# Layout of the down-projection rows, the turn of the expert product, and the order of two steps in the SSD mixer

## What is computed

```python
def expert_block(args):              # for each of the 32 experts of a layer
    xb, e = args
    hb = jax.nn.silu(xb @ w_gate[e]) * (xb @ w_up[e])   # 1024 -> 512
    return hb @ w_down[e]                               # 512 -> 1024

# end of the Mamba-2 mixer, 8 groups of 256 channels
yg = yg * lax.rsqrt(jnp.mean(yg * yg, axis=-1, keepdims=True) + RMS_EPS)
y = yg.reshape(bsz, seq, D_INNER) * norm_w
return y @ out_proj
```

## Time and profile before

| | us |
|---|---|
| median of 3 runs (lowest, highest) | 1404.52 (1402.73, 1405.75) |
| the profiled execution, its own time | 1403.31 |
| its span, first to last instruction | 1401.2 |
| busy: PE, PEld, DVE, ACT, POOL | 1093.9, 731.6, 434.8, 262.1, 6.9 |
| mean granted TensorE clock | 0.869 of 2.4 GHz |
| moved by DMA | 468.16 MB, mean 334 GB/s |

### The profile page before, as it was taken

One profiled execution on the slowest core, in us unless ns is written; L12 is line 12 of the kernel. 1 busy time (PEld: TensorE's weight loads), 2 busy tenths in 40 slices (PEclk: granted clock), 3 DMA queues, 4 the chain that ended last, 5 costly groups with the idle time before them and its releaser, 6 DMA issues.

```text
span 1401.2 us, 21348 instructions
## 1 busy us (share of the span) xinstructions
PE 1093.9 (78%) x9381; PEld 731.6 (52%) x9384; DVE 434.8 (31%) x1098; ACT 262.1 (19%) x621; POOL 6.9 (0%) x28
## 2 busy tenths in 40 slices
PE   8999786677658677679999998878667576676775
PEld 7888543443424244248888887644334242343532
DVE  2241442212212122224655554452112122222123
ACT  2210111111111111113433323211111111111112
POOL 1000000000000000000000000000000000000000
PEclk9999997978879778879999999989788787878878
DMA  9753599999999999954567652469999999999993
GB/s 345 233 221 153 238 420 423 420 420 423 419 420 422 420 420 418 417 181 124 193 225 241 228 193 98 189 265 419 419 423 420 420 423 420 419 422 420 420 410 161
DMA packets 112901, 468.16 MB, mean 334 GB/s; under 512 B 16940, under 2 KB 56104, under 8 KB 96168
## 3 DMA queue, kind: packets, MB, share of 16 engines
q1 hardware_dynamic: 112304, 466.11, 83.4%
q10 hardware_dynamic: 504, 0.67, 0.1%
HBM read 465.68 MB, written 1.08 MB: 333 GB/s over the span
## 4 chain that ended last, share of the span: by engine, by line
PE 40%; issue 36%; DMA 17%; SPq 3%; DVE 2%; ACT 1%; POOL 0%; DVEq 0%; POOLq 0%; ACTq 0%
DMA w_gu<-in_expert_w_up 15%; PE pb L1164 10%; PE pa L1164 7%; PE acc L1188 4%; PE pa L1402 4%; SPq L294 3%; DMA w_x<-in_expert_w_up 2%; PE wa L1402 2%; PE acc L1290 2%; PE wb L1411 2%; PE pb L1393 2%; PE pb L1219 1%; ACT arena L448 1%; PE wa L1171 1%; PE acc L1421 1%
## 5 line engine op out<-in xcount | busy, mean ns | idle before, releaser
L1402 PE MATMUL pa<-w_gu,arena 128*32 128x256 f32 x1536 | 131.2, 516 | 80.4 <-DMA w_gu<-in_expert_w_up 80.4
L959 DVE TENSOR_SCALAR arena<-arena 128x128 f32<-128x128 f32 x64 | 14.5, 227 | 501.6 <-ACT arena L448 501.6
L448 ACT ACTIVATE arena<-wb 32x256 f32<-32x256 f32 (+3 forms) x327 | 116.8, 357 | 230.2 <-PE wb L1485 124.6
L1402 PE MATMUL wa<-w_gu,arena 128*32 128x256 f32 x1344 | 101.2, 468 | 53.6 <-DMA w_gu<-in_expert_w_up 52.0
L1402 PEld LDWEIGHTS pa<-w_gu,arena 128*32 128x32 f32 x1536 | 61.3, 147 | 144.7 <-DMA w_gu<-in_expert_w_up 85.5
L1164 PE MATMUL pb<-hnT,w_x 128*128 128x256 f32 x512 | 113.7, 380 | 2.4 <-DVE arena L999 2.4
L1164 PEld LDWEIGHTS pb<-hnT,w_x 128*128 128x128 f32 x512 | 96.9, 191 | 15.7 <-issue 2.8
L1402 PEld LDWEIGHTS wa<-w_gu,arena 128*32 128x32 f32 x1344 | 49.0, 134 | 99.9 <-DMA w_gu<-in_expert_w_up 54.4
L1393 PE MATMUL pb<-arena,hs 128*128 128x128 f32 x480 | 74.4, 319 | 31.8 <-issue 15.1
L1393 PEld LDWEIGHTS pb<-arena,hs 128*128 128x128 f32 x480 | 68.5, 227 | 45.9 <-issue 41.2
L1411 PE MATMUL wb<-w_dn,arena 128*32 128x256 f32 x1440 | 87.0, 383 | 2.2 <-ACT arena L448 2.2
(11 more groups left out here) (278 smaller groups left out, 1216.0 us busy)
## 6 DMA issues: line engine op xcount, KB each, us to landing
w_dn<-in_expert_w_down SPq DMA_DIRECT2D x45, 2048.0 KB, 27.3
w_gu<-in_expert_w_gate SPq DMA_DIRECT2D x45, 2048.0 KB, 31.5
w_gu<-in_expert_w_up SPq DMA_DIRECT2D x45, 2048.0 KB, 30.6
arena<-in_expert_w_down SPq DMA_DIRECT2D x20, 2048.0 KB, 27.7
w_x<-in_expert_w_gate SPq DMA_DIRECT2D x20, 2048.0 KB, 32.0
w_x<-in_expert_w_up SPq DMA_DIRECT2D x20, 2048.0 KB, 30.5
w_x<-in_odd_in_proj SPq DMA_DIRECT2D x16, 1024.0 KB, 5.4
w_x<-in_odd_in_proj SPq DMA_DIRECT2D x16, 512.0 KB, 5.5
```

The source lines that it names most:

```text
L448: return nc.scalar.activation(*a, **k)
L1402: ins = mm(gu[32 * j:32 * j + 32, :, :], xb[:, k, c0:c0 + CAP], w_gu[s][:, :, k, P * j:P * j + P], start=(k == 0), stop=(k == KC - 1))
```

## The change

The down weights are loaded as `(p j)`: partition p holds rows 4p to 4p+3. For this the product must be turned so that its row 4m+j of a block stands on partition m; DVE does it in one instruction, a transpose in 32x32 blocks of a view that takes every fourth column. PE's transpose, ACT's copy and their semaphores go, in the experts and in the overflow pass. In the SSD mixer PE does bank 0 of the output projection of unit 4 where the whole stood, and banks 1 to 3 behind the square sum of unit 6; and DVE does `odd_mix(6)` behind `odd_x_silu(7)`. Cut from the diff: the list of semaphores, the name of the PSUM view, the same new layout in `overflow_weights`, and the two lines that leave the overflow pass of ACT.

```diff
@@ -294,7 +293,7 @@
                     sp_.dma_start(w_gu[s][:, part], w.rearrange("a (p k) f -> p (a k) f", k=KC)
                                   ).then_inc((S["gu_in0"], S["gu_in1"], S["gu_in2"])[s], 16)
                 else:
-                    sp_.dma_start(w_dn[s][:, :, :], w.rearrange("a (j p) n -> p (a j) n", p=P)
+                    sp_.dma_start(w_dn[s][:, :, :], w.rearrange("a (p j) n -> p (a j) n", p=P)
                                   ).then_inc((S["dn_in0"], S["dn_in1"], S["dn_in2"])[s], 16)
 
             def overflow_weights(l):
@@ -575,11 +572,11 @@
                 for e in range(NE):
                     E = NE * l + e
                     act.wait_ge(S["gu_done"], E + 1)
+                    if E:
+                        act.wait_ge(S["h_done"], E)
                     af(eg, GU[e % 2][:, 0, :], ACT.Exp, scale=-1.0).then_inc(S["gexp"], 1)
                     if e and e != OV_AT:
                         outputs_of(l, e - 1)
-                    act.wait_ge(S["ht_done"], E + 1)
-                    af(hT, HT_ps, ACT.Copy).then_inc(S["ht_copied"], 1)
                     if e == OV_AT - 1:
                         outputs_of(l, e)
                         act.wait_ge(S["table_done"], l + 1)
@@ -920,8 +917,12 @@
                 link(v.tensor_scalar(G4[b], B_ps[:, 0:SEQ], slot_id[:, :], None, ALU.is_equal))
                 v.tensor_tensor(G4[b], G4[b], B_ps[:, SEQ:], ALU.mult).then_inc(S["g4_done"], 1)
 
+            def every_fourth(a):
+
+                return a.rearrange("p (m j) -> p j m", j=FF // P)
+
             def overflow(k, l):
-                oc = Chain(dve, S["ovf_chain"], k * 8)
+                oc = Chain(dve, S["ovf_chain"], k * 9)
                 e = dve.value_load(table[0:1, ds(k + 3, 1)], min_val=0, max_val=NE - 1)
                 dve.wait_ge(S["ov_done"], k + 1)
                 oc.link(v.tensor_scalar(o_iota, iota1[:, :], ov_first[:, ds(k, 1)], None, ALU.add))
@@ -938,8 +939,9 @@
                 oc.link(v.tensor_scalar(o_eg, o_eg, 1.0, None, ALU.add))
                 oc.link(v.reciprocal(o_eg, o_eg))
                 oc.link(v.tensor_tensor(o_eg, o_eg, GU[0][:, 0, :], ALU.mult))
-                v.tensor_tensor(o_h, o_eg, GU[0][:, 1, :], ALU.mult).then_inc(S["ov_h"], 1)
-                assert oc.n == 8
+                oc.link(v.tensor_tensor(o_h, o_eg, GU[0][:, 1, :], ALU.mult))
+                v.transpose(out=o_hT, in_=every_fourth(o_h)).then_inc(S["ov_ht"], 1)
+                assert oc.n == 9
 
             def moe(l):
                 if l == 0:
@@ -959,7 +961,13 @@
                     link(v.tensor_scalar(eg, eg, 1.0, None, ALU.add))
                     link(v.reciprocal(eg, eg))
                     link(v.tensor_tensor(eg, eg, GU[e % 2][:, 0, :], ALU.mult))
+                    if E:
+                        dve.wait_ge(S["ht_done"], E)
                     v.tensor_tensor(hb, eg, GU[e % 2][:, 1, :], ALU.mult).then_inc(S["h_done"], 1)
+                    dve.wait_ge(S["h_done"], E + 1)
+                    if E:
+                        dve.wait_ge(S["dn_done"], E)
+                    v.transpose(out=hT, in_=every_fourth(hb)).then_inc(S["ht_done"], 1)
                     slot_gates(q, e, l, j)
                     if j == QUAD - 1 and q + 1 < NE // QUAD:
                         gathered(q + 1, l, 0)
@@ -1115,8 +1123,11 @@
                 if g:
                     odd_mean(g - 1)
                     odd_x_taps(g)
-                    odd_mix(g - 1)
+                    if more:
+                        odd_mix(g - 1)
                     odd_x_silu(g)
+                    if not more:
+                        odd_mix(g - 1)
                 odd_inputs(g)
                 if more:
                     odd_bc_taps(g + 1)
@@ -1174,7 +1185,7 @@
             def square_sum(a, last=False):
                 return mm(wa[0:NG + NE + 1, 0:SEQ], esum[:, :], a, start=False, stop=last, skip_group_check=True)
 
-            def out_project(m, u):
+            def out_project(m, u, banks=(0, 1, 2, 3)):
                 last = u == ODD_UNITS - 1
                 w = w_o
                 if u == ODD_UNITS - 2:
@@ -1182,7 +1193,7 @@
                     w = w_o6
                 else:
                     pe.wait_ge(S["wo_in"], (u + 1 - last) * 16)
-                for b in range(4):
+                for b in banks:
                     for i in range(2):
                         for j in range(2):
                             ins = mm(acc[:, b, 256 * i:256 * i + 256], w[:, j, 256 * b + P * i:256 * b + P * i + P],
@@ -1191,7 +1202,7 @@
                         ins.then_inc(S["eo"], 1)
                         if b:
                             logits_of(1, b - 1)
-                if not last:
+                if not last and 3 in banks:
                     ins.then_inc(S["oproj"], 1)
 
             pe.wait_ge(S["consts_pool"], 1)
@@ -1440,9 +1451,7 @@
                 pe.wait_ge(S["ov_in"], k * 48 + 48)
                 pe.wait_ge(S["ov_x"], k + 1)
                 gate_up(o_xs, 0, OV_SLOT, GU[0]).then_inc(S["ov_gu"], 1)
-                pe.wait_ge(S["ov_h"], k + 1)
-                nc.tensor.transpose(HT_ps, o_h, ident[:, :]).then_inc(S["ov_ht"], 1)
-                pe.wait_ge(S["ov_htc"], k + 1)
+                pe.wait_ge(S["ov_ht"], k + 1)
                 down(o_hT, OV_SLOT).then_inc(S["ov_dn"], 1)
                 pe.wait_ge(S["ov_yc"], k + 1)
                 combine(l, o_G4, o_y).then_inc(S["ov_done"], 1)
@@ -1450,7 +1459,9 @@
             def down_of(l, e):
                 s = SLOT[e]
                 pe.wait_ge((S["dn_in0"], S["dn_in1"], S["dn_in2"])[s], (uses(s, NE) * l + uses(s, e + 1)) * 16)
-                pe.wait_ge(S["ht_copied"], NE * l + e + 1)
+                if NE * l + e:
+                    pe.wait_ge(S["y_copied"], NE * l + e)
+                pe.wait_ge(S["ht_done"], NE * l + e + 1)
                 down(hT, s, turn=e % QUAD).then_inc(S["dn_done"], 1)
 
             def combine_of(l, q):
@@ -1479,10 +1490,6 @@
                     if j == QUAD - 1 and q + 1 < NE // QUAD:
                         gather_quad(q + 1, l, 0)
                         gather_quad(q + 1, l, 1)
-                    if E:
-                        pe.wait_ge(S["y_copied"], E)
-                    pe.wait_ge(S["h_done"], E + 1)
-                    nc.tensor.transpose(HT_ps, hb, ident[:, :]).then_inc(S["ht_done"], 1)
                     if j == 0 and q and e != OV_AT:
                         combine_of(l, q - 1)
                     if e == OV_AT - 1:
@@ -1580,19 +1587,23 @@
                     ins = mm(wb[:, 0:SEQ], ones[:, :], sq[:, j, :], start=(j == 0), stop=(j == 1))
                 ins.then_inc(S["yss_done"], 1)
 
-            def odd_out(g):
+            def odd_out(g, banks=(0, 1, 2, 3)):
                 pe.wait_ge(S["mix1_done"], g + 1)
-                out_project(mix1[g % 2], g)
+                out_project(mix1[g % 2], g, banks)
 
             for g in range(ODD_UNITS):
                 odd_scores(g)
                 odd_z(g)
                 odd_y(g)
-                if g >= 2:
+                if g == ODD_UNITS - 2:
+                    odd_out(g - 2, (0,))
+                elif g >= 2:
                     odd_out(g - 2)
                 if g + 1 < ODD_UNITS:
                     odd_x(g + 1)
                 odd_ss(g)
+                if g == ODD_UNITS - 2:
+                    odd_out(g - 2, (1, 2, 3))
                 if g + 2 < ODD_UNITS:
                     odd_bc(g + 2)
             odd_out(ODD_UNITS - 2)
```

More of the change, by code:

```diff
@@ L80 @@
 logits route_d route_e mask_done ranks table_done pos_t pg_done
-prep_sel quad_sel b_done g4_done gath_done xs_done gu_done gexp h_done ht_done ht_copied dn_done y_copied comb_part
-ov_in ov_sel ov_b ov_x ov_gu ov_exp ov_h ov_ht ov_htc ov_dn ov_yc ov_done
+prep_sel quad_sel b_done g4_done gath_done xs_done gu_done gexp h_done ht_done dn_done y_copied comb_part
+ov_in ov_sel ov_b ov_x ov_gu ov_exp ov_ht ov_dn ov_yc ov_done
 """.split()
@@ L244, in trunk_program @@
         GU = [b[:, 0:256].rearrange("p (g n) -> p g n", g=2) for b in (wa, pa)]
-        HT_ps = wb[:, 0:P]
         w_in_e = even_w_in[0].rearrange("(k p) (b m) -> p k b m", k=KC, b=6)
@@ L315, in overflow_weights @@
                         w = expert_w_down[l, ds(e, 1), :, :]
-                        sp_.dma_start(w_dn[OV_SLOT][:, :, :], w.rearrange("a (j p) n -> p (a j) n", p=P)
+                        sp_.dma_start(w_dn[OV_SLOT][:, :, :], w.rearrange("a (p j) n -> p (a j) n", p=P)
                                       ).then_inc(S["ov_in"], 16)
@@ L559, in overflow @@
                 af(o_eg, GU[0][:, 0, :], ACT.Exp, scale=-1.0).then_inc(S["ov_exp"], 1)
-                act.wait_ge(S["ov_ht"], k + 1)
-                af(o_hT, HT_ps, ACT.Copy).then_inc(S["ov_htc"], 1)
                 act.wait_ge(S["ov_dn"], k + 1)
```

## The result

| | before | after |
|---|---|---|
| median, us (lowest to highest, runs) | 1404.51 (1402.73 to 1405.75, 4) | 1379.51 (1377.48 to 1380.76, 4) |
| ratio to before, 95% interval | | 0.9822 (0.9805 to 0.9839) |
| profiled execution; its span | 1403.31; 1401.2 | 1377.48; 1375.7 |

That end is a ratio of 0.9829, which lies inside the interval of the measured one. A line of the code stands some 11 lines further down now (L1402 is L1413, L1411 L1422, L1188 L1199, L1559 L1566, L1572 L1579).

A forecast was written before the change was run, and what follows sets the result against it. The prediction took the DMA engines to bound the MoEs and PE the SSD mixer. Terms 10.1 + 1.6 + 1.1 + 7.2 = 20.0 us gave a median of 1384.5 us, range 1380.5 to 1391.7.

The forecast's parts named there:

- That end: Low end of the forecast range for the median, 1380.5 us.
- Step 1: MoE streams: down weights in 16 KB runs save 0.19 us for each of 53 parts, 10.1 us (4.8 to 13.3).
- Step 2: Turn on DVE inside the streams: one instruction of 0.29 us, costs and gains nothing there.
- Step 4: SSD mixer, split at unit 6: scores 5.55 us earlier plus 1.65 us of clock, together 7.2 us.
- the former pause: PE's 6.25 us idle before odd_scores(7) in the SSD mixer, forecast to shrink to 0.8 us.
- overflow term: Overflow pass: shorter turn there and at expert 27 brings expert 30's load earlier, 1.1 us (0.5 to 1.1).
- step 3: Turn on the path: 0.8 us at each MoE's end, 1.6 in all, plus 1.1 us at the overflow pass.
- What bounds the kernel: MoEs go at the DMA engines' pace, 14.97 us an expert at 420 GB/s; PE limits the SSD mixer.
- Row length without effect: Rival, MoE streams: 4 KB packets as good as 16 KB; other terms leave 9.9 us, 1394.6; chance 0.09.
- A new wait in the mixer: Rival, SSD mixer: odd_mix(6) behind oproj holds odd_y(7), giving back the 7.2 us, 1391.7; chance 0.09.
- PE as the bound: Rival, MoE streams: PE held at clock 0.50 becomes the limit, 93 us more, some 1488; chance 0.03.
- Layout without effect on the packets: Rival, down loads: DMA still moves 4 KB pieces, packets under 8 KB stay at 96168, 1394.6; chance 0.01.

The follow-up runs named there:

- e7: Kernel after with every expert weight part issued as two 1 MB DMAs, all runs 4 KB: 1422.7 us, ratio 1.0132.
- e5: Kernel after with the down weights again in 4 KB runs, DVE turn and SSD edits kept: 1391.4 us, ratio 0.9901.
- e8: Kernel after with every expert weight part issued as two 1 MB DMAs, all runs 8 KB: 1391.85 us, ratio 0.9903.
- e6: Kernel after with the down weights in 8 KB runs: 1385.85 us, ratio 0.9865.
- e3: Kernel before with the turn on DVE alone, down runs of 4 KB, no SSD edit: 1401.73 us, ratio 0.9988.
- e9: Kernel before again, nothing altered, one execution for its trace: 1403.84 us.
- e10: Kernel before with only the split of unit 4's output projection, odd_mix(6) left in its place: 1400.66 us, ratio 0.9962.
- e4: Kernel before with the two SSD mixer edits alone: 1397.63 us, ratio 0.9954.
- e13: Kernel after with 26 matmuls of zeros on PE ahead of each MoE's last up part: 1377.18 us, ratio 0.9802.
- e12: Kernel after with 14 matmuls of zeros on PE ahead of each MoE's last up part: 1381.21 us, ratio 0.9825.
- e14: e13 with 15 more matmuls of zeros in PE's waits ahead of the SSD mixer: 1372.61 us, ratio 0.9779.
- e1: Kernel after again, nothing altered: 1379.62 us, ratio 0.983.
- e2: Kernel before with the new down layout alone, PE's transpose kept, gate_up taking every fourth column: 1413.76 us, ratio 1.0072.

## Why the prediction missed

The mechanisms of steps 1, 2 and 4 were right. Three steps failed. The sum had no term for TensorE's clock outside the former pause; both profiles differ there by 2.8 us. Step 1 had 0.19 us for a down part, where 0.22 were measured. And the overflow term of step 3 put PE on the path in a stretch that goes at the pace of the DMA engines.

**What bounds the kernel: right.** The landings set the pace, and PE's idle time and DVE's wait for `dn_done` cost nothing. The DMA issues of after:

```profile
w_dn<-in_expert_w_down SPq DMA_DIRECT2D x45, 2048.0 KB, 26.7
```

A down part still lands 26.7 us after its issue (27.3 in rows 4), more than five times its own length: the queue stays full.

**Step 1, right mechanism, term too small.** "I take 410" for the rate behind an up part "and would take 2.097 / 426" are the readings that fell short. 427 is the rate of the all-16 KB stream, and the all-4 KB stream of e7 reads 409, which gives 5.13 - 4.91 = 0.22 us a part, as e5 to after do: (377.04 - 371.66) / 25 = 0.22 (0.215 unrounded). Over 57 parts that is 12.3 us, and the first table shows 12.6. The forecast had 10.1 for 53 of them, where 0.215 each gives 11.4, and left four to step 3. The difference is one GB/s on either side: windows of 3 and 6 us can't tell 426 from 427, and the term is itself a difference of 1.6%.

**The rules weighed in step 1.** Two rules of the Trainium skill, and both miss. "DMA: Bandwidth & Descriptors", "Specifications", with line rate from 512 B on gave 0; e7 to after is 409 to 427 GB/s between 4 KB and 16 KB. The rule of 3 cycles a packet in "Why small descriptors are slow" gave 4.7 us for the 53 parts where the measured 0.215 gives 11.4. Its form, a fixed cost of each packet, is the one that e5 to e8 show; its size isn't.

**Step 2: the cost of nothing was right, the size wrong.** The transpose takes 0.40 us, not 0.29, and lies outside the 0.25 to 0.35 named. What was missed is the price of reading every fourth column. The same instruction over all 64 experts, in after and in e5, where its input is plain (min/median/max, ns):

```profile
L970 DVE STREAM_TRANSPOSE arena<-arena x64: 401/404/425, 164.7 to 1358.4; 128x128 f32<-128x128 f32 x64
```

```profile
L970 DVE STREAM_TRANSPOSE arena<-arena x64: 311/311/314, 165.2 to 1372.6; 128x128 f32<-128x128 f32 x64
```

With every second column (e6) it is 311 ns too. At the end of MoE 0 the turn is done 0.65 us ahead of ACT's copies, and hurts nothing.

**Step 3, tails right, overflow pass wrong.** The hop gained 0.74 us in each MoE for the 0.8 forecast. The overflow pass's 1.1 us didn't come. Timeline of after:

```profile
1316.42 0.40 DVE L943 STREAM_TRANSPOSE arena<-arena 128x128 f32<-128x128 f32 x1
...
1316.88 3.47 PE L1422 MATMUL wb<-w_dn,arena 128*32 128x256 f32 x32 [2.72 <-DVE arena L943]
```

Product end to down takes 0.49 us instead of 0.90, and the down behind it 3.47 instead of 3.12 us, with the clock at 0.50 for longer: 0.06 us are left. But even a faster pass gives nothing. Expert 30 (start us, us, engine, line, operation [idle before]) in before and in e3:

```profile
1360.13 6.47 PE L1402 MATMUL wa<-w_gu,arena 128*32 128x256 f32 x64 [2.26 <-DMA w_gu<-in_expert_w_up]
```

```profile
1358.30 5.04 PE L1410 MATMUL wa<-w_gu,arena 128*32 128x256 f32 x64 [8.31 <-DMA w_gu<-in_expert_w_up]
```

In e3 PE goes from gate_up(27) to gate_up(28) in 40.9 us instead of 44.6, and then waits 8.31 us for the up part of expert 30 instead of 2.26; gate_up(27) to gate_up(31) takes 75.47 us against 75.43 (75.82 in e9). That is five experts' weights (28 to 31 and the overflow) at the stream's 15.09 us each, 75.4: in this stretch too the DMA engines set the pace, and the short dip of rows 8 costs nothing that shows. In after five times 14.87 would be 74.3, and 74.64 were measured. So the 0.8 us of this stretch belong to the rows, and some 0.3 us more may be lost in the dip.

**Step 4, right.** The pause is 0.78 for 0.8, scores 5.47 us earlier for 5.55. "The clock should stay: 1.65" was 1.55 us from scores to `odd_y(7)`, and 0.6 more came behind it, up to MoE 1. That last piece varies between 46.3 and 46.9 us among the kernels with both SSD edits (47.0 before, 47.5 in e3 and e10), so it isn't shown to be the change's. In all 7.7 by the trace for the 7.2 forecast, with 2.2 us of room for the inputs where the forecast saw 0.2; e4 alone has 7.1 by its trace and 6.2 by the medians.

**The step that is missing: TensorE's clock behind a wait.** The forecast left it at nothing everywhere but at the pause of step 4, without a reason. With the clock held (e13) each gate_up(31) takes 3.66 us; it gained 0.5 and 0.6 us from before to after. So 1.1 us of the 2.6 in the tails is the clock's return at another point of the same work. Likewise the 1.7 us ahead of the mixer. e12 to e14 show that the clock is the cause of these lengths. Whether the change shifts it is open: of the kernels without a fill there, those with the turn show 30.0 us in six profiles (after, e1, e3, e5, e7, e12), 31.7 in two (e6, e13) and 32.4 in one (e8), those without it 31.2 to 31.7 in all six. It leans to the turn, and e6 and e13 forbid to call it its effect. Both gate_up(31) together take 11.2 to 12.5 us in the kernels whose clock isn't held there (e2 left aside), in no order by kernel: 12.3 before, 11.2 after, 11.5 in e1, 12.3 in e3.

By the traces: 12.6 (rows) + 1.5 (hops) + 7.7 (mixer) = 21.7 (unrounded) for causes that the forecast named, against its 20.0, and 1.1 + 1.7 + 1.0 = 3.8 of clock and start, together 25.5 of the span. Against the forecast the rows are 1.4 more than step 1 and the overflow pass had together (12.6 for 11.2). The low end of the range took the high bound of step 1 and 0.8 for the tails, and no clock but the mixer's. The gap of 1.0 us to it is smaller than the 2.8 us of clock in these profiles, and also smaller than the scatter of the runs (1377.48 to 1380.76), so chance has a part in it.

**The rivals.** Row length without effect: excluded by e5. A new wait in the mixer: seen in e10 alone, 0.65 us. PE as the bound: not at its clock of 0.81. e2, with twice the time for each `gate_up`, shows PE late at both ends of the stream, for 9.9 us and not 84. Layout without effect on the packets: excluded by the page of the profile.

**What stays open.** The medians of e3 and e4 (2.1 + 6.2 = 8.3 us) fall short of e5 (13.1), which has both; the spans of the single profiles nearly add up (2.3 + 8.2 = 10.5, and 11.4 for e5). The profile of e3 lost 1.0 us from `odd_scores(7)` to `odd_y(7)` (10.76 for 9.71) and 0.5 behind it, and that of e4 did not have the 1.7 ahead of the mixer. Both are clock again: behind the pause the granted clock is at 0.50 for 5.3 us in e3 and 3.2 in before, and in e4 for 10.2 us ahead of the mixer as in before, where after has 6.8. Why it falls so in one kernel and not in another wasn't found.

## What to carry to other kernels

In a stream that the DMA engines bound, count packets and not only bytes: each cost 9.1 ns of one engine's time here, 1.5% of a 16 KB packet and 6% of a 4 KB one, and a transpose in blocks on an idle engine was a cheap way to longer runs, while strided matmul operands were not. A dip in the DMA share doesn't show that an engine's latency is on the path: compare the stretch with the stream's pace first. Where PE waits for a last load or a long chain, look at the granted clock behind the wait and price the work there at half rate. Where PE had nothing else to do, matmuls of zeros that reach close up to the work gave 7 us here.
